# A threshold search on VectorE beside a projection: three small operands and a scratch mask in PSUM, and stores two units later in their queue

## The chip, the cores and the metric

The kernel runs on one core of a Trainium2 chip. The metric is the device time of one execution in microseconds (us), as the median over runs. The engines that matter here are TensorE (PE, matmuls), VectorE (DVE), ScalarE (ACT), GpSimd (POOL) and SyncE (SP, which only issues DMAs here). SBUF is the large on-chip memory, PSUM the small one that matmuls write their sums to.

## The reference, cut to what matters

The program is one step of a two-layer decoder trunk over a prompt of 1024 tokens and 32 sample tokens. The change lies in the second layer, in the sparse attention. An indexer scores every key for every query, the 256 best keys of a row are kept (fewer for the samples), and attention runs over those alone:

```python
def _dsa_select(iq, iw, ik, qpos, kpos, ksel):
    r = jax.nn.relu(jnp.einsum('bthd,bsd->bhts', iq, ik, preferred_element_type=F32))
    score = jnp.einsum('bhts,bth->bts', r, iw)
    score = jnp.where(kpos[None, :] <= qpos[:, None], score, NEG)
    val, idx = lax.top_k(score, ksel)
    return idx, val > 0.5 * NEG
...
    u, q, kv, iq, ik, iw = _odd_split(h @ w_in, pos)
    o_c = _pool_mix(u, 0, pw, pb, ps)
    o_d = _dsa_prompt(q, kv, iq, ik, iw).reshape(B, T, D_Q)
```

## The kernel before, in words

**Two pieces of work in one stage.** `dsa` projects first only what the indexer needs, computes the scores (`index_scores`), and then calls `late_projections`. That stage does two things side by side: VectorE and ScalarE search for the threshold of each row, and GpSimd, TensorE and SP make the projections that the attention will want afterwards (keys, values, four tiles of queries). The stage is one block of programs, one per engine. The next stage, a rotation called "ro", starts when every engine is through with this one.

**The search.** There are seven score tiles, six for blocks of 128 prompt queries (384 to 1024 keys wide) and one for the 32 sample queries (544 wide). The threshold is built bit by bit, in 31 steps (`Selection.step`). A step sets one more bit in a candidate (`cand`, line 2582, one column for each tile), counts for every tile how many scores lie below it, compares the counts with a limit into a mask (`keep`, line 2595), and copies the candidate into the threshold where the mask says so (`thr`, line 2596). Each of these three waits for the one ahead (`link`). The counting is divided: VectorE takes the tiles of 384, 512, 896 and 544 (line 2590), ScalarE those of 640, 768 and 1024 (`signs`, line 2606). In the last of the 31 steps VectorE counts all seven. `thr`, `cand`, `count`, `keep`, `limit` and `most` are all small tiles in SBUF, 128 partitions by 7 columns.

**The projections.** There are 18 units, three chunks of 352 tokens by six weight tiles, taken chunk by chunk (`NCH` is 3, `CH` 352). A float32 product is made of three matmuls on a high and a low part of each operand, so a unit is 24 matmuls into one PSUM bank. GpSimd makes those parts: for each unit the weights (a high part, line 2352, then a low part, line 2354; `late_w_high`, `late_w_low`), and behind the weights of the first unit of a chunk also the chunk's activations in two halves (`late_x_high`, `late_x_low`, the same two lines). The weights of unit n may be split when the product of unit n-2 is done. TensorE has four PSUM banks in turn (`SLOTS`), so it begins unit n when unit n-4 is evacuated. ScalarE evacuates: unit n goes out behind its counting of step 7 + 3n/2 (rounded down), or behind the last step (line 2383). SP loads the weights (line 2341): load n waits until the weights of unit n-2 are split. It also stores the results (line 2336) from a ring of six places (`ROOM`): store n waits for the evacuation of unit n. In SP's queue the store of unit n-4 stands behind the load of unit n.

Of the kernel before, what the change touches and what calls it, by code (L numbers as in the profile page):

```python
# [14 lines left out]
U32 = mybir.dt.uint32  # L15
F32R = mybir.dt.float32r
ALU = mybir.AluOpType
# [3 lines left out]
P = 128  # L21
# [146 lines left out]
def multiply(pe, out, w, x, depth):  # L168

    for n in range(depth):  # L170
        mm = multiply_tile(pe, out, w, x, n, depth)
    return mm
# [240 lines left out]
def project_and_feed(nc, k, name, oT, w_out, row, w13, w2, out=None):  # L413
# [6 lines left out]
    with Stage(nc, name) as st:  # L420
# [57 lines left out]
        def middle(eng, step):  # L478

            step(eng, 1, 1)  # L480
            with eng.Fori(1, PAIRS // 2) as n:
                for v in range(2):
                    step(eng, 2 * n + v, v)
# [1741 lines left out]
def dsa(nc, k, idx_rows):  # L2225


    with Stage(nc, "dsa") as st:
# [17 lines left out]
        with Stage(nc, "dsal") as ld:  # L2246
# [14 lines left out]
            turn_tiles(nc, "dsat", k, [(wT[:, j * P:min((j + 1) * P, T)], iw[0:min(P, T - j * P), j]) for j in range(NT + 1)])  # L2261
        index_scores(nc, k, idx_rows, index, iw, causal, best, best_s, first, at, chosen)
        late_projections(nc, k, k.d["w_in_o"], [O_K, O_V, *range(O_Q, O_Q + 4)], k.d["po"], chosen)
        rot = st.sb("rot", [P, 5, T])
        vtok = st.sb("vtok", [P, NT, P])
# [45 lines left out]
def late_projections(nc, k, w, tiles, out, chosen):  # L2311


    SLOTS, ROOM = 4, 2 * NCH
    with Stage(nc, "late") as st:
        X, W = Split(st, "x", [P, 2, KT, CH]), Split(st, "w", [P, 2, KT, P])
        raw = k.oT[:, 4:6, 0:KT * P].rearrange("p u (n c) -> p u n c", n=KT)
        Y = k.oT[:, 6:8].rearrange("p a (c t) -> p a c t", c=NCH)
        acc = st.ps("acc", [P, SLOTS, 512])
        product, evacuated, w_high, w_split, x_high, x_split, chain_sem = map(  # L2320
            st.sem, ("product", "evacuated", "w_high", "w_split", "x_high", "x_split", "chain"))
        w_loaded, stored = st.slots("w_loaded"), st.slots("stored", ROOM)
        units = [(c, t) for c in range(NCH) for t in tiles]
        U, n_t = len(units), len(tiles)
        bits = chosen.bit
        cols = lambda c: slice(c * CH, (c + 1) * CH)
        place = lambda n: Y[:, n % ROOM // NCH, n % NCH]
        first_step = 7

        with nc.Block() as block:  # L2330
            @block.sync
            def _(sp):
                def store(n):
                    c, t = units[n]
                    sp.wait_ge(evacuated, n + 1)
                    sp.dma_start(out[t][:, cols(c)], place(n)).then_inc(stored[n % ROOM], 16)

                for n, (c, t) in enumerate(units):
                    if n >= 2:
                        sp.wait_ge(w_split, n - 1)  # L2340
                    sp.dma_start(raw[:, n % 2], w[t]).then_inc(w_loaded[n % 2], 16)
                    if n >= SLOTS:
                        store(n - SLOTS)
                for n in range(U - SLOTS, U):
                    store(n)
                for slot in range(ROOM):
                    sp.wait_ge(stored[slot], 16 * len(range(slot, U, ROOM)))

            @block.gpsimd
            def _(pool):  # L2350
                def split(high_sem, count, split_sem, src, high, low):
                    pool.tensor_scalar(high, src, chosen.one[:], 1.0, ALU.mult, ALU.mult).then_inc(high_sem, 1)
                    pool.wait_ge(high_sem, count)
                    pool.tensor_tensor(out=low, in0=src, in1=high.bitcast(F32), op=ALU.subtract).then_inc(split_sem, 1)

                for n, (c, t) in enumerate(units):
                    pool.wait_ge(w_loaded[n % 2], 16 * (n // 2 + 1))
                    if n >= 2:
                        pool.wait_ge(product, n - 1)
                    split(w_high, n + 1, w_split, raw[:, n % 2], W.high[:, n % 2], W.low[:, n % 2])  # L2360
                    if n % n_t == 0:
                        for g in range(2):
                            rows = slice(g * KT // 2, (g + 1) * KT // 2)
                            split(x_high, 2 * c + g + 1, x_split, k.xT[:, rows, cols(c)],
                                  X.high[:, c % 2, rows], X.low[:, c % 2, rows])

            @block.tensor
            def _(pe):
                for n, (c, t) in enumerate(units):
                    pe.wait_ge(w_split, n + 1)  # L2370
                    pe.wait_ge(x_split, 2 * (c + 1))
                    if n >= SLOTS:
                        pe.wait_ge(evacuated, n - SLOTS + 1)
                    multiply(pe, acc[:, n % SLOTS, 0:CH], lambda q: (W.high[:, n % 2, q], W.low[:, n % 2, q]),
                             lambda q: (X.high[:, c % 2, q], X.low[:, c % 2, q]), KT).then_inc(product, 1)

            @block.scalar
            def _(act):
                def evacuate(n):
                    act.wait_ge(product, n + 1)  # L2380
                    if n >= ROOM:
                        act.wait_ge(stored[n % ROOM], 16 * (n // ROOM))
                    act.activation(place(n), acc[:, n % SLOTS, 0:CH], ACT.Copy).then_inc(evacuated, 1)

                ready = [n for n in range(U)]
                for i in range(bits):
                    chosen.signs(act)
                    if ready and i >= first_step + 3 * ready[0] // 2:
                        evacuate(ready.pop(0))
                for n in ready:  # L2390
                    evacuate(n)

            @block.vector
            def _(dve):
                link = Chain(dve, chain_sem)
                for _ in range(bits):
                    chosen.step(dve, link)


def index_scores(nc, k, gather, index, iw, causal, best, best_s, first, at, chosen):  # L2400
# [105 lines left out]
class Selection:  # L2506
# [52 lines left out]
    def ranks(self, dve, link):  # L2559
# [12 lines left out]
        for m, r, w, score, flip, hits, on_act in self.tiles:  # L2572
            if on_act:
                link(dve.tensor_scalar(self.limit[:, m:m + 1], self.most[:, m:m + 1], 2.0, -float(w), ALU.mult, ALU.add))

    def step(self, dve, link):

        thr, cand, count, keep = self.thr, self.cand, self.count, self.keep
        self.bit -= 1
        last = self.bit == 0  # L2580
        tried = self.BITS - self.bit
        dve.tensor_scalar(cand[:], thr[:], 1 << self.bit, None, ALU.bitwise_or).then_inc(self.tried, 1)
        dve.wait_ge(self.tried, tried)
        if last and self.any_act:
            for m, r, w, score, flip, hits, on_act in self.tiles:
                if on_act:
                    link(dve.tensor_scalar(flip, score, self.sign[0:r, m:m + 1], None, ALU.mult))
        for m, r, w, score, flip, hits, on_act in self.tiles:
            if last or not on_act:
                ins = dve.tensor_scalar(hits, flip, cand[0:r, m:m + 1].bitcast(F32), None, ALU.is_lt, ALU.add,  # L2590
                                        accum_out=count[0:r, m:m + 1])
        link(ins)
        if self.any_act and not last:
            dve.wait_ge(self.signed, tried)
        link(dve.tensor_tensor(out=keep[:], in0=count[:], in1=(self.most if last else self.limit)[:], op=ALU.is_le))
        link(dve.copy_predicated(thr[:], keep[:], cand[:]))

    def signs(self, act):

# [240 lines left out]
```

## Time and profile before

| | us |
|---|---|
| median of 3 runs | 3372.27 |
| lowest and highest run | 3370.0 and 3383.53 |
| the profiled execution's own time | 3374.25 |
| span of that execution, first to last instruction | 3372.6 |

How to read the rows below. In a timeline a row is: start in us, duration in us, engine, line of the kernel, operation, output<-inputs, shape, count, and in brackets how long the engine sat idle before and what released it. Rows of the same group may be merged (x3). In a list of groups a row is: line, engine, operation, output<-inputs, shapes, count, then busy us and mean ns of one, then idle us before the group. In a view of one line, the three numbers behind the count are the shortest, median and longest duration in ns. In a table of stretches a row is: the stretch, its length, the busy us of PE, PEld (weight loads), DVE, ACT and POOL with their instructions, the granted clock of TensorE (1.00 is 2.4 GHz), the share of the DMA engines and GB/s. SPq is SP's queue of DMA issues.

The search's mask `dsa_sel_keep`, threshold `dsa_sel_thr` and candidate `dsa_sel_cand` have their names in the rows; `dsa_odd_kv` and `dsa_sel_hits` are the scores with their signs and the scratch outputs of the counting; `odd_oT` holds both the loaded weights and the results of the projection.

### The profile page before, as it was taken

Reading aid. Unit: us, or ns where it says so; the run is one execution under the profiler, and the core shown is the slowest. Engines: PE = TensorE matmul, PEld = TensorE weight load, DVE = VectorE, ACT = ScalarE, POOL = GpSimd, SP = SyncE. Lnnn points to the kernel's source line nnn. Section 1 sums busy time; section 2 is a strip of 40 time slices with the busy share of each in tenths; the row PEclk is TensorE's granted clock in tenths of the full one; section 3 lists DMA queues with packets and bytes.
Section 4 is the critical chain, followed back from the end, with each engine's and each line's share of the span. In section 5 each row is a group of like instructions: output and inputs, shape, how many; then the busy total and the mean of one; then the engine's idle time right before and its main releaser. Section 6 shows DMA issues by size and latency. Waiting matters only on the chain. (4 is left out here: it accounts for less than half of the span.)

```text
span 3372.6 us, 48761 instructions
## 1 busy us (share of the span) xinstructions
PE 3001.8 (89%) x19603; PEld 2726.0 (81%) x19603; DVE 1648.9 (49%) x2999; ACT 843.7 (25%) x1559; POOL 335.4 (10%) x294
## 2 busy tenths in 40 slices
PE   8999789987899999999996974658799999999996
PEld 8999466547799999999995953635499999999995
DVE  2111278747465434443445339977365434443445
ACT  2111167632433000000003125635333000000003
POOL 2000200005000000000000624634100000000000
PEclk9999889995799999999998977779899999999998
DMA  6222410022211111111100411210111111111101
GB/s 231 95 95 84 150 51 2 1 65 110 71 59 51 50 51 38 38 51 38 60 16 6 128 60 51 92 68 9 56 63 51 42 59 38 38 51 38 63 13 52
DMA packets 70730, 201.08 MB, mean 60 GB/s; under 512 B 12310, under 2 KB 39222, under 8 KB 61234
## 3 DMA queue, kind: packets, MB, share of 16 engines
q1 hardware_dynamic: 66674, 181.35, 15.3%
q0 software_dynamic: 2848, 11.41, 1.1%
q10 hardware_dynamic: 1008, 5.41, 0.4%
q8 instruction: 156, 2.56, 0.3%
q14 instruction: 44, 0.36, 0.0%
HBM read 167.12 MB, written 35.36 MB: 60 GB/s over the span
## 5 line engine op out<-in xcount | busy, mean ns | idle before, releaser
L163 PE MATMUL f_up<-f_x_high,f_w_first 128*128 128x352 f32 x1056 | 348.9, 330 | 21.5 <-issue 21.5
L165 PE MATMUL f_up<-f_x_high,f_w_first 128*128 128x352 f32 x1056 | 345.5, 327 | 0.0
L163 PE MATMUL f_up<-f_x_high,f_w_second 128*128 128x352 f32 x1056 | 344.7, 326 | 0.0
L164 PE MATMUL f_up<-f_x_low,f_w_first 128*128 128x352 f32 x1056 | 343.1, 325 | 0.0
L165 PE MATMUL f_up<-f_x_high,f_w_second 128*128 128x352 f32 x1056 | 342.7, 325 | 0.0
L164 PE MATMUL f_up<-f_x_low,f_w_second 128*128 128x352 f32 x1056 | 340.3, 322 | 0.0
L163 PE MATMUL f_down<-f_h_high,f_w_high 128*128 128x352 f32 x960 | 313.4, 326 | 13.9 <-issue 8.7
L165 PE MATMUL f_down<-f_h_high,f_w_low 128*128 128x352 f32 x960 | 309.8, 323 | 0.0
L164 PE MATMUL f_down<-f_h_low,f_w_high 128*128 128x352 f32 x960 | 309.6, 323 | 0.0
L870 DVE TENSOR_TENSOR f_gated<-f_silu,f_up 128x352 f32<-128x352 f32 x108 | 56.3, 521 | 516.2 <-PE f_up L165 516.2
L884 DVE TENSOR_TENSOR xT_sb<-xT_sb,f_down 128x352 f32<-128x352 f32 x384 | 198.6, 521 | 160.8 <-PE f_down L165 160.8
L163 PE MATMUL pe_acc<-pe_x_high,pe_w_high 128*128 128x352 f32 x648 | 211.2, 326 | 16.0 <-DVE pe_x_low L326 10.4
L696 ACT ACTIVATE f_silu<-f_up 128x352 f32<-128x352 f32 x108 | 50.2, 465 | 691.3 <-PE f_up L165 691.3
L163 PEld LDWEIGHTS f_up<-f_x_high,f_w_first 128*128 128x128 f32 x1056 | 201.5, 191 | 24.4 <-issue 23.8
L164 PE MATMUL pe_acc<-pe_x_low,pe_w_high 128*128 128x352 f32 x648 | 209.6, 324 | 0.0
L165 PE MATMUL pe_acc<-pe_x_high,pe_w_low 128*128 128x352 f32 x648 | 209.4, 323 | 0.0
L164 PEld LDWEIGHTS f_up<-f_x_low,f_w_first 128*128 128x128 f32 x1056 | 200.9, 190 | 0.6
L163 PEld LDWEIGHTS f_down<-f_h_high,f_w_high 128*128 128x128 f32 x960 | 180.8, 188 | 23.8 <-issue 11.3
L165 PEld LDWEIGHTS f_up<-f_x_high,f_w_first 128*128 128x128 f32 x1056 | 199.9, 189 | 0.0
L163 PEld LDWEIGHTS f_up<-f_x_high,f_w_second 128*128 128x128 f32 x1056 | 199.7, 189 | 0.2
L164 PEld LDWEIGHTS f_up<-f_x_low,f_w_second 128*128 128x128 f32 x1056 | 198.8, 188 | 0.2
L165 PEld LDWEIGHTS f_up<-f_x_high,f_w_second 128*128 128x128 f32 x1056 | 197.8, 187 | 0.0
(489 smaller groups left out, 6020.0 us busy)
## 6 DMA issues: line engine op xcount, KB each, us to landing
f_raw<-w SPq DMA_DIRECT2D x44, 1024.0 KB, 4.8
f_raw__2<-w SPq DMA_DIRECT2D x22, 1024.0 KB, 6.8
pe<-pe_y SPq DMA_DIRECT2D x27, 528.0 KB, 2.9
pe_raw<-w_in_e SPq DMA_DIRECT2D x27, 512.0 KB, 4.0
odd_oT<-w_in_o SPq DMA_DIRECT2D x18, 512.0 KB, 3.6
xT_sb<-xT ACTq DMA_DIRECT2D x4, 1056.0 KB, 11.5
po<-po_y SPq DMA_DIRECT2D x8, 528.0 KB, 2.9
y<-xT_sb SPq DMA_DIRECT2D x3, 1408.0 KB, 5.2
```

The costliest lines, as they stand in the source:

```text
L163: pe.matmul(out, wh, xh, start=n == 0, stop=False)
L164: pe.matmul(out, wh, xl, start=False, stop=False)
L165: return pe.matmul(out, wl, xh, start=False, stop=n == depth - 1)
L696: act.activation(S[:, n % 2], up[:, 0, c, 0:CH], ACT.Silu).then_inc(activated, 1)
L870: dve.tensor_tensor(out=G[:, n % 2], in0=S[:, n % 2], in1=up[:, 1, c, 0:CH], op=ALU.mult).then_inc(gated, 1)
L884: ins = dve.tensor_tensor(out=xm, in0=xm, in1=down[:, n % 2, 0:CH], op=ALU.add)
```

## The change

The stage gets one more PSUM bank, `aside`. Ahead of the first step VectorE zeroes a threshold there and copies `limit` and `most` into it (three instructions), and `thr`, `keep`, `limit` and `most` then mean these places in PSUM. `cand` and `count` stay in SBUF. Behind the last step the threshold is copied back to SBUF (one instruction). The stores in SP's queue stand `ROOM`, that is six, units behind the loads, and no longer four.

```diff
         acc = st.ps("acc", [P, SLOTS, 512])
+        aside = st.ps("aside", [P, 512])
...
                     sp.dma_start(raw[:, n % 2], w[t]).then_inc(w_loaded[n % 2], 16)
-                    if n >= SLOTS:
-                        store(n - SLOTS)
-                for n in range(U - SLOTS, U):
+                    if n >= ROOM:
+                        store(n - ROOM)
+                for n in range(U - ROOM, U):
                     store(n)
...
                 link = Chain(dve, chain_sem)
+                chosen.aside(dve, link, aside)
                 for _ in range(bits):
                     chosen.step(dve, link)
+                chosen.back(dve, link)
...
+    def aside(self, dve, link, room):
+        n = self.thr.shape[-1]
+        self.kept, at = self.thr, lambda m: room[:, m * n:(m + 1) * n]
+        thr, keep, limit, most = (at(m) for m in range(4))
+        dve.memset(thr, 0.0)
+        dve.tensor_copy(limit, self.limit[:])
+        link(dve.tensor_copy(most, self.most[:]))
+        self.thr, self.keep, self.limit, self.most = thr.bitcast(U32), keep.bitcast(U32), limit, most
+
+    def back(self, dve, link):
+        link(dve.tensor_copy(self.kept[:], self.thr))
+        self.thr = self.kept
...
-        dve.tensor_scalar(cand[:], thr[:], 1 << self.bit, None, ALU.bitwise_or).then_inc(self.tried, 1)
+        dve.tensor_scalar(cand[:], thr, 1 << self.bit, None, ALU.bitwise_or).then_inc(self.tried, 1)
...
-        link(dve.tensor_tensor(out=keep[:], in0=count[:], in1=(self.most if last else self.limit)[:], op=ALU.is_le))
-        link(dve.copy_predicated(thr[:], keep[:], cand[:]))
+        link(dve.tensor_tensor(out=keep, in0=count[:], in1=self.most if last else self.limit, op=ALU.is_le))
+        link(dve.copy_predicated(thr, keep, cand[:]))
```

On VectorE, from the end of the ranks to the second step, the rows of the kernel before are these (line 2590 is the counting):

```order
L2582 TENSOR_SCALAR dsa_sel_cand<-dsa_sel_thr 128x7
L2590 TENSOR_SCALAR dsa_odd_kv,dsa_sel_count<-dsa_odd_kv,dsa_sel_cand 128x384
L2590 TENSOR_SCALAR dsa_odd_kv,dsa_sel_count<-dsa_odd_kv,dsa_sel_cand 128x512
L2590 TENSOR_SCALAR dsa_sel_hits,dsa_sel_count<-dsa_odd_kv,dsa_sel_cand 128x896
L2590 TENSOR_SCALAR dsa_sel_hits,dsa_sel_count<-dsa_odd_kv,dsa_sel_cand 32x544
L2595 TENSOR_TENSOR dsa_sel_keep<-dsa_sel_count,dsa_sel_limit 128x7
L2596 COPY_PREDICATED dsa_sel_thr<-dsa_sel_keep,dsa_sel_cand 128x7
```

The same place in the changed kernel, whose lines are numbered later (`late_aside` is the new PSUM bank):

```order
L2585 MEMSET late_aside 128x7
L2586 COPY late_aside<-dsa_sel_limit 128x7
L2587 COPY late_aside<-dsa_sel_most 128x7
L2600 TENSOR_SCALAR dsa_sel_cand<-late_aside 128x7
L2608 TENSOR_SCALAR dsa_odd_kv,dsa_sel_count<-dsa_odd_kv,dsa_sel_cand 128x384
L2608 TENSOR_SCALAR dsa_odd_kv,dsa_sel_count<-dsa_odd_kv,dsa_sel_cand 128x512
L2608 TENSOR_SCALAR dsa_sel_hits,dsa_sel_count<-dsa_odd_kv,dsa_sel_cand 128x896
L2608 TENSOR_SCALAR dsa_sel_hits,dsa_sel_count<-dsa_odd_kv,dsa_sel_cand 32x544
L2613 TENSOR_TENSOR late_aside<-dsa_sel_count,late_aside 128x7
L2614 COPY_PREDICATED late_aside<-late_aside,dsa_sel_cand 128x7
```

The three small instructions of a step keep their places and change their operands, and three instructions stand ahead of the first step; the counting is as it was.

In SP's queue the stage begins like this in the kernel before:

```order
L2341 DMA odd_oT<-w_in_o 128x1024 x5
L2336 DMA po<-odd_oT 128x352
L2341 DMA odd_oT<-w_in_o 128x1024
L2336 DMA po<-odd_oT 128x352
L2341 DMA odd_oT<-w_in_o 128x1024
```

and like this in the changed kernel:

```order
L2342 DMA odd_oT<-w_in_o 128x1024 x7
L2337 DMA po<-odd_oT 128x352
L2342 DMA odd_oT<-w_in_o 128x1024
L2337 DMA po<-odd_oT 128x352
L2342 DMA odd_oT<-w_in_o 128x1024
```

Two more loads stand ahead of the first store, and from there on loads and stores alternate as before; seven stores, not five, stand behind the last load.

## Rows read from the trace of the kernel before

**Rows 1.** Table of stretches: the whole stage.

```profile
2055.65:2208.70 153.05, 85.64 (x432) 81.75 (x432) 148.42 (x350) 95.48 (x198) 90.61 (x48) 0.78 0.25 83
```

**Rows 2.** Groups of VectorE in this stage, shapes apart: the three small instructions.

```profile
L2582 DVE TENSOR_SCALAR dsa_sel_cand<-dsa_sel_thr 128x7 uint32<-128x7 uint32 x31 | 20.0, 646 | 1.6 <-PEq L2427 0.5
...
L2595 DVE TENSOR_TENSOR dsa_sel_keep<-dsa_sel_count,dsa_sel_limit 128x7 uint32<-128x7 f32 x30 | 18.6, 619 | 1.0
L2596 DVE COPY_PREDICATED dsa_sel_thr<-dsa_sel_keep,dsa_sel_cand 128x7 uint32<-128x7 uint32 x31 | 10.5, 338 | 1.1
...
L2595 DVE TENSOR_TENSOR dsa_sel_keep<-dsa_sel_count,dsa_sel_most 128x7 uint32<-128x7 f32 x1 | 0.2, 168 | 0.0
```

**Rows 3.** Timeline of one step with GpSimd idle.

```profile
2095.06 0.17 DVE L2582 TENSOR_SCALAR dsa_sel_cand<-dsa_sel_thr 128x7 uint32<-128x7 uint32 x1
...
2098.15 0.44 ACT L2383 ACTIVATE odd_oT<-late_acc 128x352 f32<-128x352 f32 x1
...
2098.34 0.17 DVE L2595 TENSOR_TENSOR dsa_sel_keep<-dsa_sel_count,dsa_sel_limit 128x7 uint32<-128x7 f32 x1
...
2098.75 0.17 DVE L2582 TENSOR_SCALAR dsa_sel_cand<-dsa_sel_thr 128x7 uint32<-128x7 uint32 x1
```

**Rows 4.** Timeline of the change of steps with GpSimd busy.

```profile
2111.51 1.44 POOL L2352 TENSOR_SCALAR late_x_high<-xT_sb,dsa_sel_one 128x1408 fp32r<-128x1408 f32 x1
2111.61 1.35 DVE L2595 TENSOR_TENSOR dsa_sel_keep<-dsa_sel_count,dsa_sel_limit 128x7 uint32<-128x7 f32 x1
...
2113.03 3.15 POOL L2354 TENSOR_TENSOR late_x_low<-xT_sb,late_x_high 128x1408 fp32r<-128x1408 f32 x1
2113.20 3.01 DVE L2582 TENSOR_SCALAR dsa_sel_cand<-dsa_sel_thr 128x7 uint32<-128x7 uint32 x1
...
2116.24 0.83 ACT L2606 ACTIVATE dsa_odd_kv<-dsa_odd_kv,dsa_sel_cand 128x640 f32<-128x640 f32 x1 [4.39 <-DVE dsa_sel_cand L2582]
```

**Rows 5.** Attention stage: a timeline with GpSimd busy, and the group's mean.

```profile
2289.84 2.92 POOL L1274 TENSOR_SCALAR dsaa_scores<-dsaa_scores,dsaa_weight 128x512 f32<-128x512 f32 x2 [3.21 <-DVEq L1239]
2291.62 0.56 DVE L1216 CUSTOM_DVE_ANT_0 dsaa_scores<-dsaa_scores_acc,dsa_best 128x384 f32<-128x384 f32 x1
...
L1216 DVE CUSTOM_DVE_ANT_0 dsaa_scores<-dsaa_scores_acc,dsa_best 128x384 f32<-128x384 f32 x24 | 12.4, 555 | 4.0 <-PE dsaa_scores_acc L1142 3.7
```

**Rows 6.** One line each: small copies on VectorE from PSUM, and from SBUF.

```profile
L1343 DVE COPY dsa_iw<-dsat_turn x9: 150/161/163, 1985.2 to 1986.2; 128x4 f32<-128x4 f32 x8, 32x4 f32<-32x4 f32 x1
...
L2571 DVE COPY dsa_sel_limit<-dsa_sel_most x1: 170/170/170, 2054.4 to 2054.4; 128x7 f32<-128x7 f32 x1
```

**Rows 7.** Timeline: the end of the stage.

```profile
2199.95 1.30 SPq L2336 DMA_DIRECT2D po<-odd_oT  x3
2200.10 0.17 DVE L2582 TENSOR_SCALAR dsa_sel_cand<-dsa_sel_thr 128x7 uint32<-128x7 uint32 x1
...
2208.55 0.17 DVE L2596 COPY_PREDICATED dsa_sel_thr<-dsa_sel_keep,dsa_sel_cand 128x7 uint32<-128x7 uint32 x1
2209.18 0.34 SPq L362 DMA_DIRECT2D ro_rotm<-c_rot  x1
```

**Rows 8.** Groups of GpSimd, then stretches: one unit's matmuls at either clock.

```profile
L2354 POOL TENSOR_TENSOR late_w_low<-odd_oT,late_w_high 128x1024 fp32r<-128x1024 f32 x18 | 43.0, 2387 | 1.5
L2352 POOL TENSOR_SCALAR late_w_high<-odd_oT,dsa_sel_one 128x1024 fp32r<-128x1024 f32 x18 | 20.2, 1125 | 122.7 <-DMA odd_oT<-w_in_o 112.1 <-PE late_acc L165 10.5
...
2073.00:2079.50 6.50, 6.50 (x26) 6.50 (x27) 6.36 (x18) 5.49 (x11) 3.35 (x2) 0.61 0.25 81
2079.50:2083.30 3.80, 3.80 (x25) 3.51 (x23) 3.66 (x6) 0.44 (x3) 3.52 (x2) 1.00 0.00 0
```

**Rows 9.** DMA issues, and a timeline of the slowest load with its splitter.

```profile
odd_oT<-w_in_o SPq DMA_DIRECT2D x18, 512.0 KB, 3.6
...
2143.76 0.43 SPq L2341 DMA_DIRECT2D odd_oT<-w_in_o  x1
...
2148.69 1.13 POOL L2352 TENSOR_SCALAR late_w_high<-odd_oT,dsa_sel_one 128x1024 fp32r<-128x1024 f32 x1 [1.42 <-DMA odd_oT<-w_in_o]
```

## The prediction, made before the changed kernel was run

> **What bounds the kernel now.** I read the table of stretches first, to find the stage that the change touches and the engine that is never free in it. The whole stage lasts 153.05 us, and VectorE is busy for 148.42 of them, TensorE for 85.64, ScalarE for 95.48, GpSimd for 90.61 [rows 1]. The end of the stage confirms it: TensorE's results are gone with the last stores, issued from 2199.95 on, while VectorE is still at its last step; its last instruction ends at 2208.72, and the next stage's first DMA is issued at 2209.18 [rows 7]. So the search on VectorE sets the stage's end, and what it loses or gains moves all that follows.
>
> Then the groups of VectorE, where a mean far above the quiet duration is what the reader should see. The three small instructions of a step work on 7 columns. They take 646, 619 and 338 ns on average, but 168 ns in the one row that runs when GpSimd is through [rows 2]. The timelines say why. With GpSimd idle each takes 0.17 us, and a step takes 3.69 us, from the candidate at 2095.06 to the next at 2098.75 [rows 3]. With GpSimd busy the mask starts at 2111.61 and ends at 2112.96, as GpSimd's instruction does (2111.51 + 1.44); the next candidate starts at 2113.20 and ends at 2116.21, where GpSimd's next one ends (2113.03 + 3.15 = 2116.18) [rows 4]. ScalarE, which needs the candidate for its part of the counting, sat idle for 4.39 us there. These small instructions wait out the GpSimd instruction that they fall on.
>
> **What the waits are worth.** Busy time of the three is 20.0 + 18.6 + 0.2 + 10.5 = 49.3 us for 93 instructions [rows 2]; alone they would take 93 x 0.17 = 15.8 us [rows 3]. The difference is **33.5 us** of waiting, all on the path. As a cross-check by steps: 30 quiet steps of 3.69 and a last one of 8.62 (2200.10 to 2208.72) [rows 7] make 119.3 us, 33.7 less than the stage's 153.05.
>
> **Does moving operands to PSUM end the wait?** In the candidate's instruction the one input is then in PSUM, in the mask's one of two, in the copy the mask and the output, with the candidate still in SBUF. The nearest row is in the attention stage: an instruction of VectorE with one input in PSUM and one in SBUF, 128x384. One of these starts at 2291.62 while GpSimd works until 2292.76, and takes 0.56 us; the mean of 24 is 555 ns, with GpSimd busy beside many of them [rows 5]. It doesn't wait. I take all 33.5 us as removed. The Trainium skill says the same in "SBUF — State Buffer", section "Who interferes with whom": VectorE and GpSimd share a second pair of SBUF ports, held for a whole instruction, and a VectorE instruction with two SBUF inputs, or one in a two-port mode, needs it, but not one with at most one SBUF input outside those modes. The traces above agree with both halves of it.
>
> **What is added.** Three instructions ahead of the first step and one behind the last. Two of the small ones with their gap take 0.41 us (2098.34 to 2098.75) [rows 3], so 0.2 each: 0.8 us, all on the path. They run before GpSimd's first split or after its last, so nothing is there to wait for.
>
> **What PSUM costs.** No VectorE instruction of this trace writes PSUM. Reading it has a row: a copy of 4 columns from PSUM takes 161 ns at the median, a copy of 7 columns within SBUF 170 [rows 6], so reading costs nothing that shows (the lower end: -0.01 us an instruction). As the upper end I take that an instruction takes twice its 0.17 us. I am nearest to the read row and take 0.03 us for each of the 93, as two of the three also write: **2.8 us**; the ends are -0.9 and 15.8. The Trainium skill speaks against this change here: "Perfetto Trace Analysis", section "Optimizing Scalar/DVE Operations", gives VectorE about 60 ns of access overhead on SBUF and about 125 on PSUM. An estimate from that page is 93 x 0.065 = 6.0 us in place of my 2.8, and a time of 3345.5; the read row doesn't show such a difference.
>
> **The sum.** 33.5 - 0.8 - 2.8 = 29.9, so 30 us. A step is then 3.69 + 0.09 = 3.78 us.
>
> **What is late next.** ScalarE evacuates unit n behind its counting of step 7 + 3n/2. If the product isn't ready, ScalarE stands, its counting of the next step comes late, and the search waits for it. So I compare both at the first unit of each chunk. The search: unit 0 goes out at 2055.65 + 0.6 + 7 x 3.78 + 3.2 = 2085.9 (3.2 is the counting, as 2095.06 to 2098.15 shows [rows 3]), and 9 steps are 34.0 us, so units 6 and 12 follow at 2119.9 and 2153.9. The feed: unit 0 is done at about 2079.5, after 6.5 us at a mean clock of 0.61 [rows 8]. From there to the first product of the next chunk are four units at full clock (3.8 us each [rows 8], 15.4 with their starts), one split of weights (1.12 + 2.39 + 0.08 between = 3.6), the chunk's activations (2 x (1.44 + 3.15 + 0.08) = 9.3 [rows 4]) and a first unit that again runs partly at 1.2 GHz, since TensorE stood idle through the split (6.8): 35.1 us, so 2114.6 and 2149.7. The room is 6.4, 5.3 and 4.2 us. It shrinks but lasts: the other five units of the last chunk are done by 2169, the search's last step begins at 2169.7, and it runs 8.7 us with the remaining evacuations and stores beside it. ScalarE's evacuation itself fits in a step: it ends at 2098.59, before the candidate of 2098.75 [rows 3].
>
> **The stores.** Worth nothing in this sum. Load n stands behind the store of unit n-5 now, and behind that of n-7 then. The tightest load is that of unit 12, wanted when product 10 is done, at 2114.6 + 15.4 = 2130. In the old order it would wait for the evacuation of unit 7 at 2124 and land 3.6 us later [rows 9], in time. In the new order it waits for the split of unit 10 alone. A load lands 3.6 us after its issue at the median and 4.9 at the worst (2143.76 to 2148.69 [rows 9]), while GpSimd splits for 3.6 the unit between: up to 1.3 us per unit are open, and the room covers them. In evacuations nothing is held: unit n needs the store of n-6, which stands behind load n, long issued by then. I give the order 0 to 1 us.
>
> **Everything behind the stage** starts at its end by a barrier and loads its own data, so it shifts by 30 us.
>
> **The rivals.** (1) *The feed becomes the bound.* If loads land late and the first unit of a chunk and the next both run at 1.2 GHz (about 3.2 us more), the room of 4.2 us is used up, and each us beyond it goes to the search. With 5 us lost, the gain is 25: 3347. For: the feed's chain of 35.1 us per chunk is longer than the search's 34.0. Against: the room at the start. (2) *PSUM is dear*: at 0.17 us an instruction the gain is 33.5 - 0.8 - 15.8 = 16.9: 3355.4. Against it is the read row. The figure of the page cited above lies between this and the forecast. (3) *One of the three still waits.* The candidate is still written to SBUF, from a single input; if that one keeps its 20.0 - 31 x 0.17 = 14.7 us, the gain is 15.2: 3357. Against: in the row with one PSUM input the output goes to SBUF too [rows 5]. (4) *Slower: the waits stay, and PSUM comes on top.* If the second input of mask and copy still goes the way that GpSimd blocks, and a candidate read from PSUM waits as well, nothing is gained, and 0.8 + 93 x price is lost: 3372.3 at no price, 3389 at 0.17. It passes 0.5% from 0.18 us an instruction (17.5 us: 3389.8).
>
> **How the numbers follow.** The profiled execution took 3374.25 us, 1.65 over its span and 2.0 over the median of 3372.27. The sum stands against it: 3374.25 - 30 = 3344.3, and so a median of **3342**. This forecast, with a PSUM price from nothing to 0.1 us, runs from 3340 to 3349, and has 0.84; rivals 1 to 4 have 0.04 each. The range begins at 3337, the upper gain of 32.7 less the 2.3 us by which the lowest run lies under the median, and reaches over rival 1 towards rival 2, to 3354; outside are most of rivals 2 to 4, about 0.1. What a measurement of this kernel can tell from no change is about 0.5%, 17 us. Faster by more: the forecast, rival 1 and half of rival 2, 0.90. Within it: the rest of 2, rival 3 and half of 4, 0.08. Slower: 0.02.
>
> **What would show it.** Right: the three small instructions at 0.2 us or less on average, with GpSimd's splits beside them as long as before; a quiet step and a busy one alike at about 3.8 us; the stage at about 123 us; ScalarE never waiting for a product. Wrong: any of the three with a mean near its old one (rivals 3 and 4), all three evenly at 0.25 or more (rival 2), ScalarE's evacuation released by TensorE at units 12 and 13 (rival 1), or a later stage that is longer than before by what this one lost.

## The result, and the profile after

| | before, us | after, us |
|---|---|---|
| median of 3 runs | 3372.27 | 3339.88 |
| lowest and highest run | 3370.0 and 3383.53 | 3332.01 and 3343.9 |
| the profiled execution's own time | 3374.25 | 3332.01 |
| its span | 3372.6 | 3330.4 |

After runs at 0.9891 of before, with a 95% interval of 0.9847 to 0.9936. Set against the 3372.27 of before that is 3335.5 us: 36.8 us gained, between 22 and 52 by the interval. From median to median it is 32.4 us. The prediction had 30, and its range ended at 3337, so the ratio lies 1.5 us under the range, although the median as it stands, 3339.88, lies in it. Three runs leave that much open; the five later ones below put the gain at 38.8. Direction and mechanism came as forecast; the gain was larger.

The first view is the stage in the table of stretches of after. It answers [rows 1], which ends at VectorE's last instruction; this row ends at the next stage's first DMA, and for before that stage is 2055.65 to 2209.18, 153.53 us [rows 7].

```profile
2050.30:2171.49 121.19, 77.49 (x432) 74.77 (x432) 115.48 (x354) 95.62 (x198) 91.00 (x48) 0.81 0.34 105
```

The stage is 32.3 us shorter. VectorE loses 32.9 us of busy time with four instructions more; ScalarE and GpSimd do what they did, in the same busy time to 0.4 us. So what went was waiting inside VectorE's instructions. The groups of VectorE in this stretch name the ones (they answer [rows 2]; the last two are the mean of one instruction each, ahead of the first step):

```profile
L2614 DVE COPY_PREDICATED late_aside<-late_aside,dsa_sel_cand 128x7 uint32<-128x7 uint32 x31 | 5.4, 174 | 1.1
L2613 DVE TENSOR_TENSOR late_aside<-dsa_sel_count,late_aside 128x7 uint32<-128x7 f32 x31 | 5.3, 171 | 1.1
...
L2600 DVE TENSOR_SCALAR dsa_sel_cand<-late_aside 128x7 uint32<-128x7 uint32 x31 | 5.1, 166 | 1.1
...
L2587 DVE COPY late_aside<-dsa_sel_most 128x7 f32<-128x7 f32 x1 | 0.2, 157 | 0.0
L2585 DVE MEMSET late_aside<- 128x7 f32 x1 | 0.1, 64 | 0.6 <-PEq L2430 0.6
```

Candidate, mask and copy took 646, 619 and 338 ns; now they take 166, 171 and 174. Busy time of the three is 15.8 us, which is 93 x 0.17: nothing of the waits is left, and PSUM adds nothing that can be seen. GpSimd's splits beside them are as long as before (2387 ns [rows 8]), as its first group of after shows:

```profile
L2355 POOL TENSOR_TENSOR late_w_low<-odd_oT,late_w_high 128x1024 fp32r<-128x1024 f32 x18 | 43.3, 2406 | 1.5
```

The timeline of after at the place that answers [rows 4], the first activations of the second chunk:

```profile
2097.30 1.44 POOL L2353 TENSOR_SCALAR late_x_high<-xT_sb,dsa_sel_one 128x1408 fp32r<-128x1408 f32 x1
...
2098.58 0.17 DVE L2613 TENSOR_TENSOR late_aside<-dsa_sel_count,late_aside 128x7 uint32<-128x7 f32 x1
2098.79 0.17 DVE L2614 COPY_PREDICATED late_aside<-late_aside,dsa_sel_cand 128x7 uint32<-128x7 uint32 x1
2098.82 3.19 POOL L2355 TENSOR_TENSOR late_x_low<-xT_sb,late_x_high 128x1408 fp32r<-128x1408 f32 x1
2098.99 0.17 DVE L2600 TENSOR_SCALAR dsa_sel_cand<-late_aside 128x7 uint32<-128x7 uint32 x1
2099.19 0.83 ACT L2624 ACTIVATE dsa_odd_kv<-dsa_odd_kv,dsa_sel_cand 128x640 f32<-128x640 f32 x1 [0.72 <-DVE dsa_sel_cand L2600]
...
2102.68 0.17 DVE L2600 TENSOR_SCALAR dsa_sel_cand<-late_aside 128x7 uint32<-128x7 uint32 x1
```

The mask (line 2613) starts 0.16 us before GpSimd's instruction ends and takes 0.17 us, not 1.35; the candidate lies wholly beside the next one, of 3.19 us, and takes 0.17, not 3.01. ScalarE waits 0.72 us for the candidate, not 4.39. The step is 2098.99 to 2102.68, 3.69 us, the same as the quiet step of before [rows 3]. It is so throughout: in before, 30 of the 93 small instructions take over 0.2 us, and each of the 30 starts inside a GpSimd instruction and ends within 0.04 us of that instruction's end; in after, 65 of the 93 run wholly inside a GpSimd instruction, and none takes over 0.174 us.

The end of the stage, the timeline that answers [rows 7]:

```profile
2163.83 0.46 ACT L2384 ACTIVATE odd_oT<-late_acc 128x352 f32<-128x352 f32 x1 [1.89 <-PE late_acc L165]
...
2170.21 0.17 DVE L2614 COPY_PREDICATED late_aside<-late_aside,dsa_sel_cand 128x7 uint32<-128x7 uint32 x1
2170.41 0.17 DVE L2591 COPY dsa_sel_thr<-late_aside 128x7 uint32<-128x7 uint32 x1
2171.49 0.34 SPq L362 DMA_DIRECT2D ro_rotm<-c_rot  x1
```

ScalarE waits for a product once in the whole stage, 1.89 us at the last unit, with 6.5 us of VectorE's last step still to run behind it. The search still sets the end, but the feed now ends only that far ahead of it.

### The profile page after: what moved, and what is told of

It reads as the page before. It is cut to its first block and busy times, and to the rows that moved or that the text cites. A ratio compares the mean times of both kernels' runs of the same rounds, so it can differ in the third digit from the quotient of the medians.

```text
span 3330.4 us, 48765 instructions
## 1 busy us (share of the span) xinstructions
PE 2984.3 (90%) x19603; PEld 2710.9 (81%) x19603; DVE 1613.0 (48%) x3003; ACT 843.8 (25%) x1559; POOL 337.7 (10%) x294
```

## The experiments

**The theory:** each of the three small VectorE instructions, two of which take two inputs from SBUF while the third goes from SBUF to SBUF with one source, is held until the GpSimd instruction ends that it falls on; with one of its inputs moved to PSUM it passes. **The rivals:** the order of the stores makes the gain, or part of it; not PSUM but the new tiles or their place makes it; one of the three operands is the one that counts, and the others only follow it; the chance places at which steps fall on GpSimd's instructions set how much is lost, in before too. The quoted texts give the theories letters and say what each expects. In what follows "waits" is the busy time of the 93 small instructions beyond 0.17 us each, and the stage goes from its first weight load to the next stage's first DMA; both are from each kernel's profile.

| kernel | stage, us | waits, us | stage's start | behind the stage |
|---|---|---|---|---|
| before, the profile above | 153.53 | 33.4 | 2055.65 | 1163.4 |
| before, twice more | 156.83, 157.10 | 36.7, 37.0 | 2046.65, 2047.90 | 1163.6, 1162.9 |
| after, the profile above | 121.19 | 0 | 2050.30 | 1158.9 |
| after, twice more | 121.18, 121.23 | 0 | 2048.18, 2047.19 | 1165.1, 1160.7 |
| PSUM alone | 121.18 | 0 | 2048.58 | 1164.5 |
| stores alone | 151.98 | 31.9 | 2051.92 | 1165.0 |
| the same code, scratch in SBUF | 152.81 | 31.6 | 2055.20 | 1161.6 |
| mask and limits in PSUM, threshold in SBUF | 134.71 | 14.2 | 2041.53 | 1161.1 |
| threshold in PSUM, mask and limits in SBUF | 135.67 | 15.2 | 2041.24 | 1162.7 |
| before, GpSimd's splits in pieces | 147.76 | 27.7 | 2048.83 | 1164.8 |
| after, three products moved to ScalarE | 118.72 | 0 | 2044.87 | 1163.9 |

**After, again.** The changed kernel, without an edit, beside the experiments that start from it.

> The changed kernel again, to size the gain and to see how much of the distance between two profiles lies outside the stage. Theory A (all 33.5 us of waits went, PSUM costs nothing an instruction): stage 121 us, gain 32 to 33 us, ratio 0.990. Theory B (the change also helps outside its stage): gain 37 or more, with the part from the stage's end to the program's end some 4 us shorter than before again. By A those stretches outside scatter either way.

The median is 3336.31 us over 5 runs (3328.09 to 3340.92), 0.9885 of before (0.9865 to 0.9905, before being 3375.18 over 17 runs). A further single run took 3330.76. The gain, 38.8 us, is above A's 32 to 33, and the stretch behind the stage, 1165.1 us, isn't shorter than that of before, as B has it: neither text fits whole.

> The changed kernel once more, for a third profile. Theory H: stage 121.2 us to 0.1 us, the stretches outside it scatter as the others do.

The stage repeats to 0.05 us in three profiles: without the waits nothing in it depends on chance.

**PSUM alone.** On the changed kernel, the old order of the stores.

```diff
-                    if n >= ROOM:
-                        store(n - ROOM)
-                for n in range(U - ROOM, U):
+                    if n >= SLOTS:
+                        store(n - SLOTS)
+                for n in range(U - SLOTS, U):
```

> The PSUM part alone; stores four units behind the loads as before. Theory A (the stores are worth nothing, VectorE bounds the stage): stage 121 us, the same time as the whole change within 3 us. Rival C (the stores gave the 2 us that the forecast missed, since loads held up by stores starve the feed): stage 123 us or more, and ScalarE's evacuations wait for TensorE at units 6, 7, 12 or 13.

3338.92 us over 5 runs, 0.9899 (0.9882 to 0.9917), and a stage of 121.18 us, the same to 0.01. The waits of ScalarE for a product, by line:

```profile
ACT odd_oT L2384 <- PE late_acc L165: 2.1, 1, 2.1
```

One wait at the last unit, as in after. With the search at 3.69 us a step the old order holds no load long enough to matter: GpSimd waits for a load once, for the first. The order is worth nothing that these runs can tell. The ratios of this kernel and of after, 0.9899 and 0.9885, lie within each other's intervals.

**Stores alone.** On the kernel before, the reverse of that edit.

```diff
-                    if n >= SLOTS:
-                        store(n - SLOTS)
-                for n in range(U - SLOTS, U):
+                    if n >= ROOM:
+                        store(n - ROOM)
+                for n in range(U - ROOM, U):
```

> The store part alone, all small tiles in SBUF. Theory A: the splits on GpSimd come earlier and closer together, the three small instructions wait for them as before, 30 to 36 us in all; stage 150 to 157 us, time within 0.2% of before. Rival C: stage 150 us or less, gain of 3 us or more.

3372.42 us over 12 runs, 0.999 (0.9975 to 1.0004). The order does work on GpSimd. Its waits by what it waited for, first of before, then of this kernel, are:

```profile
POOL late_w_high L2352 <- DMA odd_oT<-w_in_o: 112.1, 10, 82.8
POOL late_w_high L2352 <- PE late_acc L165: 10.5, 5, 3.6
```

```profile
POOL late_w_high L2352 <- DMA odd_oT<-w_in_o: 82.8, 1, 82.8
POOL late_w_high L2352 <- PE late_acc L165: 31.4, 14, 6.0
```

In before nine loads besides the first came late, for 29.3 us together. With the new order none does, but GpSimd then waits for TensorE instead, and GpSimd doesn't set the end. The small instructions of VectorE stay as they were:

```profile
L2582 DVE TENSOR_SCALAR dsa_sel_cand<-dsa_sel_thr 128x7 uint32<-128x7 uint32 x31 | 20.0, 644 | 1.6 <-PEq L2427 0.5
...
L2595 DVE TENSOR_TENSOR dsa_sel_keep<-dsa_sel_count,dsa_sel_limit 128x7 uint32<-128x7 f32 x30 | 18.7, 622 | 1.0
```

**The same code with the scratch in SBUF.** This keeps everything of the change, the added instructions and the new tiles too, but not the place.

```diff
-        aside = st.ps("aside", [P, 512])
+        aside = st.sb("aside", [P, 28])
```

> The changed kernel with its scratch tile in SBUF and not in PSUM: the same instructions, the same four more of them, the same stores. Theory A (PSUM is what matters): waits of 30 to 36 us, stage 151 to 158 us, time within 0.3% of before. Rival F (the new layout, all four small tiles in one, or the order of stores gives the gain): stage near 121 us.

3371.48 us over 10 runs, 0.9988 (0.9974 to 1.0001). The gain is gone and the waits are back, 31.6 us of them. Groups of VectorE in its stage, with the names of after:

```profile
L2613 DVE TENSOR_TENSOR late_aside<-dsa_sel_count,late_aside 128x7 uint32<-128x7 f32 x31 | 20.0, 646 | 1.1
...
L2600 DVE TENSOR_SCALAR dsa_sel_cand<-late_aside 128x7 uint32<-128x7 uint32 x31 | 18.8, 607 | 1.1
L2614 DVE COPY_PREDICATED late_aside<-late_aside,dsa_sel_cand 128x7 uint32<-128x7 uint32 x31 | 8.6, 278 | 1.1
```

So it is the memory that these tiles lie in, and nothing else of the change, that gives the gain.

**Mask and limits in PSUM, the threshold in SBUF.** On the changed kernel; the candidate is then read from SBUF again, as its only input, and written there.

```diff
...
-        thr, keep, limit, most = (at(m) for m in range(4))
-        dve.memset(thr, 0.0)
+        keep, limit, most = (at(m) for m in range(1, 4))
         dve.tensor_copy(limit, self.limit[:])
         link(dve.tensor_copy(most, self.most[:]))
-        self.thr, self.keep, self.limit, self.most = thr.bitcast(U32), keep.bitcast(U32), limit, most
+        self.thr, self.keep, self.limit, self.most = self.thr[:], keep.bitcast(U32), limit, most
...
     def back(self, dve, link):
-        link(dve.tensor_copy(self.kept[:], self.thr))
-        self.thr = self.kept
+        pass
```

> The mask and the two limits in PSUM, the threshold still in SBUF. So the mask's instruction and the copy have one SBUF input each, and the candidate is made from SBUF into SBUF. Theory A (it is each instruction's own operands that decide): the mask and the copy at 0.17 us, the candidate waiting alone with a mean of 0.65 us or more, 15 to 22 us of waits; stage 137 to 143 us, gain 10 to 18 us. Rival D (it is enough to have one of the three out of SBUF, the others then pass): gain near 30 us. Rival E (a copy whose output lies in SBUF waits although it has one SBUF input): waits of 25 us or more.

3346.61 us over 6 runs, 0.9927 (0.9908 to 0.9946). Groups of VectorE in its stage:

```profile
L2596 DVE TENSOR_SCALAR dsa_sel_cand<-dsa_sel_thr 128x7 uint32<-128x7 uint32 x31 | 19.5, 628 | 1.1
...
L2609 DVE TENSOR_TENSOR late_aside<-dsa_sel_count,late_aside 128x7 uint32<-128x7 f32 x31 | 5.3, 171 | 1.1
L2610 DVE COPY_PREDICATED dsa_sel_thr<-late_aside,dsa_sel_cand 128x7 uint32<-128x7 uint32 x31 | 5.3, 170 | 1.1
```

The candidate alone still waits, 14.2 us over the 31, a little under the text's 15 to 22. Mask and copy pass with one of their two inputs in PSUM, although the copy writes SBUF here. The stage, 134.71 us, is a little shorter than the text had it, and the gain is larger than its 10 to 18: 18.8 to 22.4 us by the stages of before, 24.6 by the ratio.

**The threshold in PSUM, mask and limits in SBUF.** The complement.

```diff
-        self.kept, at = self.thr, lambda m: room[:, m * n:(m + 1) * n]
-        thr, keep, limit, most = (at(m) for m in range(4))
-        dve.memset(thr, 0.0)
-        dve.tensor_copy(limit, self.limit[:])
-        link(dve.tensor_copy(most, self.most[:]))
-        self.thr, self.keep, self.limit, self.most = thr.bitcast(U32), keep.bitcast(U32), limit, most
+        self.kept = self.thr
+        thr = room[:, 0:n]
+        link(dve.memset(thr, 0.0))
+        self.thr, self.keep, self.limit, self.most = thr.bitcast(U32), self.keep[:], self.limit[:], self.most[:]
```

> The threshold alone in PSUM; mask and limits in SBUF. The candidate then has one input, in PSUM, and its output in SBUF; the mask's instruction has two SBUF inputs, the copy two as well, with its output in PSUM. Theory A: the candidate at 0.17 us; mask and copy wait, 15 to 25 us together; stage 137 to 146 us. Rival D (one of the three is enough): stage near 121 us. Rival E (the output's place decides): the copy passes at 0.17 us, the candidate waits.

One run, 3341.26 us. Groups of VectorE in its stage:

```profile
L2609 DVE TENSOR_TENSOR dsa_sel_keep<-dsa_sel_count,dsa_sel_limit 128x7 uint32<-128x7 f32 x30 | 17.2, 573 | 1.0
L2610 DVE COPY_PREDICATED late_aside<-dsa_sel_keep,dsa_sel_cand 128x7 uint32<-128x7 uint32 x31 | 8.5, 276 | 1.1
...
L2596 DVE TENSOR_SCALAR dsa_sel_cand<-late_aside 128x7 uint32<-128x7 uint32 x31 | 5.1, 166 | 1.3 <-DVE late_aside L2583 0.3
```

Now the candidate passes, and mask and copy wait, 12.1 and 3.2 us. The copy's output lies in PSUM here, and that doesn't save it: its two inputs in SBUF hold it. The stage, 135.67 us, is again a little shorter than the text had it. Each half of the change frees the instructions that the theory names, and no other; neither half carries the gain by itself.

**Before, with GpSimd's splits in pieces.** Each split is cut into instructions of two tiles, four times as many for the weights and twice for the activations, with the same data. If a small instruction waits for the end of the one GpSimd instruction that it falls on, its longest wait must shrink to the longest piece.

```diff
-                    pool.tensor_scalar(high, src, chosen.one[:], 1.0, ALU.mult, ALU.mult).then_inc(high_sem, 1)
+                    pieces = src.shape[1] // 2
+                    cut = lambda a, i: a[:, 2 * i:2 * i + 2]
+                    for i in range(pieces):
+                        ins = pool.tensor_scalar(cut(high, i), cut(src, i), chosen.one[:], 1.0, ALU.mult, ALU.mult)
+                    ins.then_inc(high_sem, 1)
                     pool.wait_ge(high_sem, count)
-                    pool.tensor_tensor(out=low, in0=src, in1=high.bitcast(F32), op=ALU.subtract).then_inc(split_sem, 1)
+                    for i in range(pieces):
+                        ins = pool.tensor_tensor(out=cut(low, i), in0=cut(src, i), in1=cut(high, i).bitcast(F32), op=ALU.subtract)
+                    ins.then_inc(split_sem, 1)
```

> The kernel before with GpSimd's instructions cut into pieces of two tiles each (four for weights, two for a half of the activations), the same work in the same order. Theory A (a waiting instruction waits for the end of the one GpSimd instruction that it fell on): no wait longer than about 1.6 us, the longest piece, where the candidate had 3.0; sum of waits between 15 and 28 us, since an instruction that got through meets the next piece sooner. Rival G (GpSimd's activity slows these instructions however long its own are): sum of waits as before, 33 us.

One run, 3363.06 us. The candidate and the copy in before (shortest, median and longest in ns), the same two here, and GpSimd's longest piece:

```profile
L2582 DVE TENSOR_SCALAR dsa_sel_cand<-dsa_sel_thr x31: 170/171/3009, 2055.7 to 2200.1; 128x7 uint32<-128x7 uint32 x31
```

```profile
L2596 DVE COPY_PREDICATED dsa_sel_thr<-dsa_sel_keep,dsa_sel_cand x31: 170/171/1383, 2059.4 to 2208.5; 128x7 uint32<-128x7 uint32 x31
```

```profile
L2588 DVE TENSOR_SCALAR dsa_sel_cand<-dsa_sel_thr x31: 170/432/803, 2048.9 to 2187.5; 128x7 uint32<-128x7 uint32 x31
```

```profile
L2602 DVE COPY_PREDICATED dsa_sel_thr<-dsa_sel_keep,dsa_sel_cand x31: 171/430/1595, 2052.6 to 2196.0; 128x7 uint32<-128x7 uint32 x31
```

```profile
L2359 POOL TENSOR_TENSOR late_x_low<-xT_sb,late_x_high 128x704 fp32r<-128x704 f32 x12 | 19.8, 1674 | 0.5
```

The longest of the three kinds is the copy's 1.6 us, where the candidate of before reached 3.0 [rows 4], and the longest piece is 1.67. Again every instruction over 0.2 us ends within 0.04 us of a piece's end, so it is the end of a GpSimd instruction that they wait for, and rival G falls. But 65 of the 93 take over 0.2 us, where 30 did: the medians of candidate and copy rise from 171 to 432 and 430 ns (the mask's falls from 517 to 274), and GpSimd is busy for 113.52 us and not 90.6. The waits fall to 27.7 us only. Shorter instructions bound each wait and leave most of the sum.

**Before, twice more.** No edit. These settle whether 33.4 us of waits were a low sample, and whether the 8 us that the first profile of before lost in an early stage belong to the kernel.

> The kernel before, profiled again. Its stage is 32.3 us longer than the changed one's in the first profiles, but the runs lie 34 to 39 us apart. Theory H (the rest is scatter of a part that the change doesn't touch, and the stage before is as long in every run): stage 152 to 155 us again, the stretch ahead of the stage anywhere between 2041 and 2056 us. Theory I (the first profile of the kernel before had a lucky stage; its waits depend on how the steps fall on GpSimd's instructions): stage 157 us or more. Theory J (the kernel before loses some 8 us early in the program that the others don't, as in its first profile between 72 and 103 us): the same loss again at the same place.

> The kernel before once more, for a third profile: the same three theories, with the same numbers.

The first is 3376.60 us over 10 runs, against before 1.0005 (0.9991 to 1.002); the second is one run, 3369.53. The stage rows of the two:

```profile
2046.65:2203.48 156.83, 87.38 (x432) 83.54 (x432) 151.70 (x350) 95.52 (x198) 90.48 (x48) 0.77 0.25 81
```

```profile
2047.90:2205.00 157.10, 85.34 (x432) 81.49 (x432) 151.95 (x350) 95.54 (x198) 90.52 (x48) 0.79 0.25 81
```

The stages are 3.3 and 3.6 us longer than the 153.53 of the first profile, with the same work: not the 152 to 155 of theory H, and I's 157 to within 0.2. The groups of VectorE in the first of them show where:

```profile
L2595 DVE TENSOR_TENSOR dsa_sel_keep<-dsa_sel_count,dsa_sel_limit 128x7 uint32<-128x7 f32 x30 | 20.3, 678 | 1.1
...
L2582 DVE TENSOR_SCALAR dsa_sel_cand<-dsa_sel_thr 128x7 uint32<-128x7 uint32 x31 | 17.0, 548 | 1.6 <-PEq L2427 0.5
L2596 DVE COPY_PREDICATED dsa_sel_thr<-dsa_sel_keep,dsa_sel_cand 128x7 uint32<-128x7 uint32 x31 | 15.0, 485 | 1.1
```

The waits fall on other instructions than in [rows 2] (548, 678 and 485 ns, where there were 646, 619 and 338) and come to 36.7 us; in the other profile it is 709, 705 and 306, and 37.0 us. One execution is one draw of where 93 small instructions meet 48 of GpSimd.

The early loss of the first profile of before isn't repeated, so theory J falls. Its rows, as stretches and then TensorE's timeline, are:

```profile
71.93:87.76 15.83, 10.26 (x66) 9.97 (x64) 1.92 (x2) 1.39 (x3) 0.00 (x0) 0.90 0.58 234
87.76:95.40 7.64, 7.64 (x37) 7.64 (x38) 1.92 (x2) 0.46 (x1) 0.00 (x0) 0.76 0.31 99
```

```profile
87.72 0.66 PE L163 MATMUL pe_acc<-pe_x_high,pe_w_high 128*128 128x352 f32 x1 [5.57 <-DVE pe_w_low L157]
```

TensorE stood for 5.57 us and then ran at the 1.2 GHz level for a while (a matmul of 0.66 us, where the one at 81.83, ahead of the gap, took 0.32; the granted clock of the stretch from 87.76 is 0.76). The next stage's first DMA came at 333.84, where the twelve other profiles have 325.6 to 326.0. The two spans shown differ by 42.2 us: 32.3 in the stage, 5.4 ahead of it, where this loss stands, and 4.5 behind it.

**After, with the last step's three products on ScalarE.** The end of the stage shows VectorE alone: in the last step it first multiplies three score tiles by their signs, then counts all seven, while ScalarE has only evacuations left. Here ScalarE makes the three products and VectorE counts its own four tiles meanwhile.

```diff
-        if last and self.any_act:
-            for m, r, w, score, flip, hits, on_act in self.tiles:
-                if on_act:
-                    link(dve.tensor_scalar(flip, score, self.sign[0:r, m:m + 1], None, ALU.mult))
-        for m, r, w, score, flip, hits, on_act in self.tiles:
+        order = sorted(self.tiles, key=lambda t: t[-1]) if last else self.tiles
+        for m, r, w, score, flip, hits, on_act in order:
+            if last and on_act:
+                dve.wait_ge(self.signed, tried)
...
+        if self.act_bit == 0:
+            act.wait_ge(self.signed, self.BITS - 1)
+            for m, r, w, score, flip, hits, on_act in self.tiles:
+                if on_act:
+                    ins = act.activation(flip, score, ACT.Copy, scale=self.sign[0:r, m:m + 1])
+            ins.then_inc(self.signed, 1)
             return
```

> The changed kernel, and ScalarE, idle in the last step, renews the three signed score tiles that VectorE renews there itself (2.0 us on the path), while VectorE counts its own four first. If the search on VectorE is still what ends the stage: last step 6.7 us, stage 119 us, 2 us faster than the changed kernel, which this measurement can't tell from none but the profile can. If the feed or the stores now end the stage: no change in its length.

3331.17 us over 5 runs (3325.61 to 3343.82), 0.9883 of before (0.9861 to 0.9905). The timeline of its last step:

```profile
2156.07 2.68 ACT L2624 ACTIVATE dsa_odd_kv<-dsa_best,dsa_sel_sign 128x640 f32<-128x640 f32 x3
...
2156.34 0.17 DVE L2600 TENSOR_SCALAR dsa_sel_cand<-late_aside 128x7 uint32<-128x7 uint32 x1
...
2162.75 0.17 DVE L2613 COPY_PREDICATED late_aside<-late_aside,dsa_sel_cand 128x7 uint32<-128x7 uint32 x1
```

From the candidate to the end of the copy it is 6.6 us (2156.34 to 2162.92), where the last step of before took 8.6 [rows 7]. After's last step takes 8.6 as well (2161.76 to 2170.38). The stage is 118.72 us, 2.5 less than after's: 2.0 in the last step, and 0.45 between VectorE's last instruction and the next stage's first DMA, a place that this edit doesn't touch. In the runs 0.9883 can't be told from after's 0.9885, so the gain over after is one of the profile alone.

## Why the prediction was right, and where it was off

**Right: what bounds the stage, and that the waits go whole.** The search set the end before and sets it now. Candidate, mask and copy each pass when one of their inputs lies in PSUM; the two halves of the change, and the scratch in SBUF, show that it is this and for each of the three. Rivals 3 and 4 fell with that: a candidate that still waited would have left a stage of about 135 us (it did, where it was made to), and the stage is 121.19. The rule that the prediction took from the Trainium skill, "SBUF — State Buffer", section "Who interferes with whom", agrees with the halves as well: one input from SBUF passes (171 and 170 ns), two wait (573 and 276), and the candidate, a single source from SBUF to SBUF, waits (628), as the rule has it for a two-port mode; in which mode it ran, no trace shows.

**Right: the stores are worth nothing here** (0 to 1 us in the prediction). Alone they give 0.999 (0.9975 to 1.0004), and without them the stage stays at 121.18. That they end nine late loads of before and still give nothing is the point: GpSimd then waits for TensorE.

**Right: the four added instructions, 0.8 us.** In the trace of after the three ahead of the first step go from 2050.39 to the candidate at 2051.01, and the one behind the last adds 0.2. But the stage less its waits grew by 1.1 us (120.1 to 121.2): the next stage's first DMA now also follows VectorE's last instruction by 0.91 us and not by 0.46 [rows 7]. Why, no run shows.

**Off: the waits, 33.5 us.** This is the step that failed: not the mechanism, but the size of this term and its range. It was read rightly from one execution, but two others of the same kernel waited 36.7 and 37.0 us, 35.7 on the mean of the three. The mean of the three stages of before is 155.8 us, and 34.6 us more than after's; with the two later ones alone it is 35.6 and 35.9. The prediction treated as a property of the kernel what was a draw, and gave the term no range at all, though [rows 3] and [rows 4] already held a hint: equal instructions that take from 0.17 to 3 us, depending on where they fall. The forecast of 30 us misses by this term, 2.2 us on the mean, and by the next, 2.8; the range allowed for the next one and not for this one.

**Off: the price of PSUM, 2.8 us.** It measured nothing: 166, 171 and 174 ns against 170, 168 and 171 in SBUF, and a step of 3.69 us against 3.69. The row that the prediction called nearest [rows 6] had said so; the 0.03 us was added for writing, and writing costs 3 ns. Rival 2, a dear PSUM, fell. The Trainium skill's "Perfetto Trace Analysis", section "Optimizing Scalar/DVE Operations", from which the prediction worked out an estimate of 6.0 us, isn't borne out for instructions of 7 columns in this chain.

**Off: the range's lower end, 3337.** It took the largest gain to be 32.7 us, the whole of one execution's waits less 0.8. With 37.0 us of waits the end would have been some 3.5 us lower, and the 3335.5 of the ratio would have been in it. (Two slips in the working have no bearing on that: by the prediction's own lower end for PSUM the largest gain is 33.6, not 32.7, and rival 4 at no price is 3373.1, with its 0.8 added, not 3372.3.)

**Half right: the room of the feed.** It was forecast at 6.4, 5.3 and 4.2 us for units 0, 6 and 12. It measured 6.8, 4.0 and 2.2. The last of these is read from GpSimd's split of unit 14's weights, which TensorE releases at the end of product 12, and the evacuation of unit 12:

```profile
2144.20 1.13 POOL L2353 TENSOR_SCALAR late_w_high<-odd_oT,dsa_sel_one 128x1024 fp32r<-128x1024 f32 x1 [2.68 <-PE late_acc L165]
...
2146.37 0.44 ACT L2384 ACTIVATE odd_oT<-late_acc 128x352 f32<-128x352 f32 x1
```

The feed's chain was sized well, 35.9 and 35.1 us a chunk where 35.1 stood; the search came faster than forecast, 33.2 us for nine steps and not 34.0, since PSUM costs nothing. So rival 1, the feed as the bound, didn't come, but it is nearer than the prediction had it: 2.2 us at unit 12, and a wait of 1.89 at the last.

**What stays open.** The stage is 32.3 to 35.9 us shorter, 34.6 on the mean of the three profiles of before; the runs say 36.8, and in five more runs 38.8 (3375.18 x 0.0115). The difference of 2 to 4 us lies in no place that these profiles single out. What lies ahead of the stage and behind it, and is the same code in all kernels, varies by itself: the stage starts between 2041.2 and 2055.7, and the rest takes 1158.9 to 1165.1, in 13 profiles. The intervals (0.002 of the time, about 7 us, to each side in the runs of five) cover it, and no run here resolves it.

## What to carry to other kernels

Where small VectorE instructions sit in a serial chain beside a busy GpSimd, look at the longest of a group against its shortest: if it matches the rest of a GpSimd instruction, put inputs into PSUM, so that each instruction reads at most one tensor from SBUF, and one that has a single source reads that from PSUM; do it for every instruction of the chain that waits. Which ones wait has to be read from the trace: the counting too goes from SBUF to SBUF with one tensor as its source, and it doesn't wait. Its first group, in before and in after:

```profile
L2590 DVE TENSOR_SCALAR_CACHE_REDUCE dsa_odd_kv<-dsa_odd_kv,dsa_sel_cand 128x384 f32<-128x384 f32 x31 | 19.0, 612 | 1.3 <-DVE dsa_sel_cand L2582 0.3
```

```profile
L2608 DVE TENSOR_SCALAR_CACHE_REDUCE dsa_odd_kv<-dsa_odd_kv,dsa_sel_cand 128x384 f32<-128x384 f32 x31 | 19.0, 612 | 1.1
```

The shortest takes 611 ns in both. Whether a single-source instruction also passes when only its output lies in PSUM, no run shows.

Waits of this kind are a draw from execution to execution, so size the term from several profiles, or give it the range of one. A DMA order that ends late loads is worth only what the engine that waited for them is worth.

## What was not expected of the hardware

A tiny operand doesn't spare an instruction these waits: 7 columns, 0.17 us of work, took up to 3.0 us for a GpSimd instruction of 3.15 [rows 4], and 1.6 when the longest piece was 1.67. For the conditional copy it is the two inputs that decide and not the output: with both in SBUF and the output in PSUM it took 276 ns on average, with the mask in PSUM and the output in SBUF 170. Writing PSUM from VectorE at this size costs 3 ns more than writing SBUF (171 and 174 ns against 168 and 171). And the same kernel lost 33.4, 36.7 and 37.0 us to the waits in three executions, while the kernel without them repeats its stage to 0.05 us.
